# Modulation's products packed four at a time into 32-column blocks of TensorE

## The reference, cut to what matters

```
sc, scc = silu(c), silu(c_ctx)                        # 1024 each
for l in range(2):
    shift, scale, gate = split(sc @ mod_w[l] + mod_b[l], 3)       # mod_w[l] is 1024 x 3072
    hx = rmsnorm(x, norm_g[l]) * (1 + scale) + shift
    if l == 0:
        shift_c, scale_c, gate_c = split(scc @ mod_w[l] + mod_b[l], 3)
        hc = rmsnorm(ctx, norm_g[l]) * (1 + scale_c) + shift_c
    ...                                               # mixers of layer l read hx (and hc)
```

## Time and profile before

| | us |
|---|---|
| median of 3 runs | 3279.63 (3277.35 to 3283.79) |
| the profiled execution | 3278.73 |
| its span, first to last instruction | 3276.8 |
| stage "start", until the first projection product | 116.66 |
| busy in the span: PE, DVE, ACT, POOL | 3032.7, 1777.4, 1088.6, 1274.3 |

### The profile page before, as it was taken

One profiled execution on the slowest core, in us unless ns is written; L12 is line 12 of the kernel. 1 busy time (PEld: TensorE's weight loads), 2 busy tenths in 40 slices (PEclk: granted clock), 3 DMA queues, 4 the chain that ended last, 5 costly groups with the idle time before them and its releaser, 6 DMA issues.

```text
span 3276.8 us, 39932 instructions
## 1 busy us (share of the span) xinstructions
PE 3032.7 (93%) x13850; PEld 2299.9 (70%) x13850; DVE 1777.4 (54%) x2304; ACT 1088.6 (33%) x1414; POOL 1274.3 (39%) x1546
## 2 busy tenths in 40 slices
PE   7999999988989998989889999998999999998997
PEld 1588777756768877767677877776666666665775
DVE  2499999975363415363622232445455555556353
ACT  3244334433120100000322232224455556655332
POOL 0244445436634434436423233675211212121575
PEclk9999999999999999999899999999999999998999
DMA  8212111254311131113211112333321122111323
GB/s 328 93 55 77 61 61 61 69 175 144 122 52 52 46 141 46 47 37 122 84 59 33 32 34 88 96 89 113 71 52 34 39 52 46 46 39 39 129 81 112
DMA packets 101654, 258.43 MB, mean 79 GB/s; under 512 B 24513, under 2 KB 25601, under 8 KB 99985
## 3 DMA queue, kind: packets, MB, share of 16 engines
q1 hardware_dynamic: 71824, 189.43, 19.6%
q10 hardware_dynamic: 29696, 67.21, 5.7%
HBM read 223.97 MB, written 32.64 MB: 78 GB/s over the span
## 4 chain that ended last, share of the span: by engine, by line
PE 62%; DVE 16%; issue 9%; ACT 6%; POOL 4%; DMA 2%; DVEq 1%; SPq 0%; POOLq 0%; ACTq 0%
PE ps L577 16%; PE ps L578 15%; PE ps L579 15%; DVE ps L1927 4%; POOL t_wl L535 3%; PE ps L1065 2%; PE ps L665 2%; DVE t_tt L1872 1%; PE ps L1082 1%; POOL t_wh L530 1%; PE ps L879 1%; PE ps L881 1%; PE ps L880 1%; DVE t_pr L2386 1%; PE ps L1102 1%
## 5 line engine op out<-in xcount | busy, mean ns | idle before, releaser
L577 PE MATMUL ps<-t_h_hi,t_wh 128*128 128x512 f32 x2464 | 1017.4, 413 | 76.3 <-POOLq L538 38.9
L530 POOL CAST t_wh<-t_wst 128x1024 fp32r<-128x1024 f32 (+2 forms) x306 | 329.5, 1077 | 1861.0 <-PE ps L579 1659.0
L578 PE MATMUL ps<-t_h_lo,t_wh 128*128 128x512 f32 x2464 | 985.3, 400 | 0.0
L579 PE MATMUL ps<-t_h_hi,t_wl 128*128 128x512 f32 x2464 | 984.6, 400 | 0.0
L535 POOL TENSOR_TENSOR t_wl<-t_wst,t_wh 128x256 fp32r<-128x256 f32 (+2 forms) x1224 | 938.5, 797 | 24.5
L577 PEld LDWEIGHTS ps<-t_h_hi,t_wh 128*128 128x128 f32 x2464 | 471.4, 191 | 227.3 <-issue 100.4
L578 PEld LDWEIGHTS ps<-t_h_lo,t_wh 128*128 128x128 f32 x2464 | 471.5, 191 | 113.8 <-issue 8.7
L579 PEld LDWEIGHTS ps<-t_h_hi,t_wl 128*128 128x128 f32 x2464 | 470.0, 191 | 114.6
L1927 DVE SCALAR_TENSOR_TENSOR ps<-t_upad,t_vec,ps 128x1024 f32<-128x1024 f32 x224 | 274.7, 1284 | 6.6 <-DVE ps L1921 0.9
L577 PE MATMUL ps<-t_y_hi,t_wh 128*128 128x512 f32 x512 | 207.9, 406 | 24.7 <-DVEq L265 14.6
L578 PE MATMUL ps<-t_y_lo,t_wh 128*128 128x512 f32 x512 | 206.1, 402 | 0.0
(11 more groups left out here) (339 smaller groups left out, 4289.7 us busy)
## 6 DMA issues: line engine op xcount, KB each, us to landing
t_modw<-w_mod SPq DMA_DIRECT2D x12, 2048.0 KB, 8.3
t_wst<-w_even_in SPq DMA_DIRECT2D x40, 512.0 KB, 3.5
t_wst<-w_ple SPq DMA_DIRECT2D x64, 320.0 KB, 2.9
t_wst<-w_even_out SPq DMA_DIRECT2D x32, 512.0 KB, 3.6
t_wst<-w_fox_in SPq DMA_DIRECT2D x32, 512.0 KB, 3.6
t_xr<-x_d ACTq DMA_DIRECT2D x6, 2048.0 KB, 11.4
t_wst<-w_gla_in SPq DMA_DIRECT2D x24, 512.0 KB, 3.8
t_wst<-w_odd_in_a SPq DMA_DIRECT2D x16, 512.0 KB, 3.5
```

Of the source, the lines that this page charges most:

```text
L530: pool.tensor_copy(wh[b][:, 0:w], wst[b][:, 0:w]).then_inc(S("w_high"), 1)
L577: pe.matmul(o, w1, x1, start=start and k == 0, stop=False)
L578: pe.matmul(o, w1, x2, start=False, stop=False)
L579: last = pe.matmul(o, w2, x1, start=False, stop=stop and k == kts - 1)
```

## The change

The stationary operand becomes `silp`: 32 columns per k-tile, of which the first two hold silu(c) and silu(c_ctx) and the other 30 are zero. The product of k-tile k goes to the column block j = 32 * (k % 4) of TensorE and so to partitions j to j+31 of the bank; k-tiles 0 to 3 start the sums of their block, 4 to 7 end them. The bank then holds four partial sums for each of the two rows, at partitions 32 i and 32 i + 1. ScalarE copies all 128 partitions. The turn is no longer a transpose but a product of the 128 x 128 piece of `mrow` with `four` (128 x 2, ones at partitions 32 i of column 0 and 32 i + 1 of column 1), which sums the four parts as it turns them. VectorE clears `silp` and builds `four` from slices of the identity; PE waits for the latter.

```
 silp = sb("silp", 32 * KT, MISC + 47 * KB)
 four = sb("four", 2, MISC + 47 * KB - 32)
...
         pe.wait_ge(S("silc"), 1)
+        pe.wait_ge(S("consts"), 2)
...
                 for k in range(KT):
-                    at = (c % 3) * 4096 + k * HALF
-                    last = pe.matmul(bank(2 + c % 2)[0:2, :], silc[:, 2 * k:2 * k + 2], modw[:, at:at + HALF],
-                                     start=(k == 0), stop=(k == KT - 1))
+                    at, j = (c % 3) * 4096 + k * HALF, 32 * (k % 4)
+                    last = pe.matmul(bank(2 + c % 2)[j:j + 32, :], silp[:, 32 * k:32 * k + 32], modw[:, at:at + HALF],
+                                     start=(k < 4), stop=(k >= 4), tile_position=(0, j))
                 last.then_inc(S("mod_used"), 1)
...
                 for q in range(4):
-                    last = pe.transpose(bank(layer, 2 * (m + q), 2 * (m + q) + 2),
-                                        mrow[(c - 1) % 2][0:2, q * P:(q + 1) * P], ident[0:2, 0:2])
+                    last = pe.matmul(bank(layer, 2 * (m + q), 2 * (m + q) + 2),
+                                     mrow[(c - 1) % 2][:, q * P:(q + 1) * P], four[:, :], start=True, stop=True)
...
-        A(silc[:, :], V("c", 0, 16), ACT.Silu).then_inc(S("silc"), 1)
+        A(silp[:, :].rearrange("p (k m) -> p k m", m=32)[:, :, 0:2],
+          V("c", 0, 16).rearrange("p (k v) -> p k v", v=2), ACT.Silu).then_inc(S("silc"), 1)
...
-            A(mrow[c % 2][0:2, :], bank(2 + c % 2)[0:2, :], ACT.Copy).then_inc(S("mod_row"), 1)
+            A(mrow[c % 2][:, :], bank(2 + c % 2), ACT.Copy).then_inc(S("mod_row"), 1)
...
+        line.go(dve.memset(silp[:, :], 0.0))
         line.sync()
         dve.sem_inc(S("consts"), 1)
         dve.wait_ge(S("vec_loaded"), 16)
+        line(TT_(four[:, :], ident[:, 0:2], ident[:, 32:34], ALU.add))
+        for j in range(2, 4):
+            line(TT_(four[:, :], four[:, :], ident[:, 32 * j:32 * j + 2], ALU.add))
+        dve.sem_inc(S("consts"), 1)
```

More of the change, by code:

```diff
@@ L136, in build @@
     gsc = sb("gsc", 32, sm + 384)
-    silc = sb("silc", 16, sm + 512)
     sp8 = sb("sp8", 16, sm + 576)
@@ L403, in build @@
     mrow = [sb(f"mrow{i}", HALF, R1 + (48 + 2 * i) * KB) for i in range(2)]
+    silp = sb("silp", 32 * KT, MISC + 47 * KB)
+    four = sb("four", 2, MISC + 47 * KB - 32)
     @block.sync
```

## The result

| | before | the change |
|---|---|---|
| median (range) | 3278.49 us (3277.03 to 3283.79, 4 runs) | 3256.93 us (3253.71 to 3259.94, 4 runs) |
| ratio, 95% interval | | 0.9931 (0.9914 to 0.9948) |
| span of the profiled execution | 3276.8 | 3258.0 |
| stage "start" in that execution | 116.66 | 98.46 |
| the rest of it | 3160.1 | 3159.5 |

Forecast were 3265 us, within 3253 to 3273. The time lies inside the range, but it is the time of the first rival, packing by four (3257), not of the case that I held likeliest. Timed again in a later job, the ratio was 0.9945 (0.993 to 0.9961); one of the five executions there took 5817 us, with TensorE's passes at half speed, and is left out of the ratio. The traces put 18.2 us of gain into the stage (116.66 - 98.46) and 0.6 into the rest; the first four runs' 21.6 have some luck of the runs in them.

A forecast was written before the change was run, and what follows sets the result against it. Loads until 33 us, ACT until 51, then PE's series were taken to bound the stage; chunks of 4.75 us for 7.30, with waits and a 5.33 us tail, put the projection at 102.4, gain 14.2, 3265 us, range 3253 to 3273.

The forecast's parts named there:

- the first rival: Modulation products: four blocks run at once, 16 passes in 4 slots, 1.7 us; gain 22 us, to 3257; chance 0.28.
- the case that I held likeliest: Modulation products overlap by two: nine slots a chunk instead of 16, projection at 102.4, kernel 3265 us; chance 0.45.
- What bounds the stage: Stage before the first projection, 116.66 us: loads until 33, ACT until 51, PE's series after it, DVE close behind.
- The price of a chunk: Chunk of modulation products: 9 slots of 0.43, 3.87 us, plus a turn of 0.88; 4.75 us for 7.30.
- The turn: Turn after each chunk: eight small passes of 0.11 us, 0.88 us for 0.34, bounds 0.68 to 1.52.
- The start of chunk 4: After the column sums, begun 0.76 us earlier, and row 2: chunk 4 starts near 52.0 us, for 52.15.
- The clock: PE's pause of some 3 us before 51 brings half clock: 1.4 us added to chunk 4, ends 0 and 3.9.
- The tail: From PE's last chunk to the first projection: row, high and low part take 5.33 us, unchanged.
- Covers: Side work costs nothing: loads (chunk 7's close, 1 or 2 us if late), wider copy, clearing, building `four`, POOL's split.
- The slower side: Modulation products slower than before if weight loads can't hide below another block's running pass; chance of slower 0.08.
- bare loads: Rival for modulation products: each of 16 passes has its load in front, 9.5 us a chunk, 3297 us; chance 0.08.
- no overlap: Rival: blocks take turns on the moving stream, 7.76 us a chunk, 3 to 7 us slower, 3283; chance 0.14.

The follow-up runs named there:

- e2: The changed kernel with k-tiles alternating between two column blocks, packing by two instead of four; 3264.0 us, ratio to before 0.9961.
- e3: The changed kernel with the same four column blocks, but adjacent k-tiles (0 and 1, 2 and 3, and so on) in one block; 3260.19 us, ratio to before 0.9945.
- e4_warm: The changed kernel with products that nobody reads added in PE's pauses; 3251.54 us, ratio to before 0.9929.
- e1: The changed kernel with all eight k-tiles of a chunk in column block 0, so without the packing; 3284.92 us, ratio to before 1.0021.
- e6_rows_early: The changed kernel with ScalarE's row copies 6 to 10 placed earlier among its normalised tiles, no unread products; 3258.5 us, ratio to before 0.9946.

## Why the prediction came out as it did

- **What bounds the stage**: right in the main. In the change it is loads to 33, ScalarE to about 49, PE to 62, then DVE's tiles to 80 and PE again. I had read PE's series as the only path before, from 51 on; that chain, too, runs through DVE's first tiles and row 6 (75.39 to 82.04).
- **The price of a chunk**, the step that failed: "a pass waits while its own block is busy" is right, "passes start in order" is not. Products are 4 slots, 1.85 us for my 3.87. e2 shows that with a price near mine the end comes out 1.7 us from where I put it, and e3 that another order costs the same. The rival's 1.7 us was right.
- **The number**: that the time lies in the range is no merit of the case that I held likeliest, since the range was drawn to hold this rival too. And that it meets the rival's 3257 is in part luck: the rival had the projection at 94.5, it came at 98.46, and runs that gained 3.4 us more than the stage (21.6 for 18.2) made up for it.
- **The turn**: 0.98 for 0.88 at full clock, right; at half clock 1.8, which I did not count.
- **The start of chunk 4**: 51.19 for 52.0. The sums started at 38.06, not 41.5, for the first of them needs only the squares of `x` (done at 36.39) and PE, which a turn held until 38.06; only the context's sum needs what I had both wait for. At half clock the sums took 3.56 for 1.82 and the turn after them 1.79 for 0.88, which gave 2.6 of these 3.4 back.
- **The clock**: mis-sized. I added 1.4 us for chunk 4 alone. It hit the sums, turn 2, products 4, turn 6, products 8, and nearly all from turn 8 on; e4_warm puts 5 to 6.6 us on it. This is why packing by four ended at 98.5 and not at the rival's 94.5: at full clock the work after row 8 would have ended near 89.5 (81.88 and 7.6 us of turns and products), and the context, ready at 90.14, would have bound, as the rival had it.
- **The tail**: 5.33 us from the last product's end to the projection became 5.8 (92.69 to 98.46), for the turns in it take longer.
- **Covers**: the wider copy (0.60 us), clearing (0.27) and building `four` (0.51) cost nothing. Chunk 7's load was the close one, as I had it: PE waited 0.98 us for it (to 62.82), off the path. That GpSimd's split would come to lie on VectorE's context I had not seen; in the change it cost 2.4 us of VectorE (5.11 for 2.67), all hidden.
- **The slower side**: bare loads are refuted by the four passes that start together; no overlap is what e1 builds, and it costs about what I said (3 to 7 us; measured 7 to 8 by the runs, 6.3 by the stage).

The rule of the Trainium skill weighed ahead ("TensorE: Matmul & The Clock Gate", The mechanism: loads below running products only where the row groups differ, or into the background buffer) holds here only by its second half: eight loads are made within the first 0.2 us, four of them for blocks whose pass is running. Of its section Measured speedup vs the span model (2.38 times for three blocks), this case has the like for two and four, 6.99 / 3.56 = 1.96 and 6.99 / 1.85 = 3.8.

## What to carry to other kernels

A float32 product with few stationary columns can be packed into 32-column blocks at nearly full return, in either of the two orders tried, but the sum over the blocks has its price, here 0.64 us a chunk. When a change thins out PE's work, cost the pauses it opens: the work left may run at half clock, and here that took back 5 to 7 us. Then ask which engine's order now paces PE, and what comes to lie beside what.

## What the runs showed of the hardware

Unread products in PE's pauses made the stage shorter by 5 to 6.6 us. VectorE's 128 x 256 float32 `tensor_scalar` takes 0.33 us start to start alone and over twice that while GpSimd works on SBUF (0.80 on average in e6_rows_early). The rest of the kernel, which no experiment touches, took between 3153 and 3167 us in single profiled executions (span less the stage: 3153.3 in e4_warm, 3166.9 in e1_one_block); it goes with the granted clock there. By the clock's record 197 us of the rest ran at the lower level in e4_warm and 228 in e1_one_block; half of that difference is 15 us, and the rests differ by 13.6. What makes the clock fall more often in one execution than in another is not shown, and it is why a difference of a few us between these kernels stays open.
